# Scores of 64-wide heads read 64 rows instead of 128 zero-padded ones, and a norm is placed earlier among the top-k rounds

## Time and profile before

| | |
|---|---|
| median of three runs | 2206.35 us (2206.09 to 2206.84) |
| the profiled execution | 2206.82 us |
| its span in the trace | 2205.0 us |
| TensorE matmuls busy | 2140.5 us (97%), mean granted clock 0.993 |
| TensorE weight loads busy | 1748.2 us (79%) |
| VectorE busy | 1294.4 us (59%) |
| ScalarE busy | 871.9 us (40%) |
| GpSimd busy | 162.4 us (7%) |

### The profile page before, as it was taken

The page is one execution under the profiler, slowest core; times in us unless marked ns, Lnnn a source line. Parts: engine busy times, 40 slices in busy tenths (PEclk is TensorE's granted clock), DMA queues, the critical chain, the costliest instruction groups (busy, mean ns, idle before and its releaser), DMA issues.

```text
span 2205.0 us, 31360 instructions
## 1 busy us (share of the span) xinstructions
PE 2140.5 (97%) x10498; PEld 1748.2 (79%) x10498; DVE 1294.4 (59%) x2291; ACT 871.9 (40%) x1659; POOL 162.4 (7%) x96
## 2 busy tenths in 40 slices
PE   7998999999999999999999999999999999999997
PEld 6577778888888878888888888888888887777775
DVE  7887555666643566466666435555544457556663
ACT  4444453322223266533322332222222355455652
POOL 0042001000001111020000122000000110000001
PEclk9999999999999999999999999999999999999998
DMA  4122102233333311123332333333233334300002
GB/s 161 48 87 59 57 29 86 96 96 99 99 96 105 103 41 38 42 94 105 95 95 95 99 111 96 95 95 96 96 102 97 95 89 133 104 20 20 20 11 76
DMA packets 49472, 180.83 MB, mean 82 GB/s; under 512 B 5488, under 2 KB 5616, under 8 KB 49264
## 3 DMA queue, kind: packets, MB, share of 16 engines
q1 hardware_dynamic: 49248, 179.25, 26.0%
q0 software_dynamic: 144, 0.52, 0.1%
HBM read 177.66 MB, written 2.10 MB: 82 GB/s over the span
## 4 chain that ended last, share of the span: by engine, by line
PE 83%; DVE 4%; ACT 3%; issue 2%; DVEq 0%; POOLq 0%; ACTq 0%; POOL 0%
PE pj L2178 69%; PE po L2540 3%; PE ps L2500 2%; PE po L2395 2%; PE pt L2515 2%; PE ps L2349 2%; PE pt L2365 1%; DVE rtmp L1437 1%; ACT w_both L716 1%; DVE s_sb L1490 1%; PE pj L2318 1%; PE po L2404 0%; PE ps L2489 0%; ACT pT L830 0%; DVE w_both L1300 0%
## 5 line engine op out<-in xcount | busy, mean ns | idle before, releaser
L2178 PE MATMUL pj<-h_hi,w_both 128*128 128x512 f32 x3472 | 1121.8, 396 | 17.1 <-DVE w_both L1300 13.7
L2178 PEld LDWEIGHTS pj<-h_hi,w_both 128*128 128x128 f32 x3472 | 653.9, 188 | 156.8 <-issue 16.1
L2178 PE MATMUL pj<-h_lo,w_both 128*128 128x512 f32 x1736 | 677.4, 390 | 0.0
L716 ACT ACTIVATE w_both<-raw 128x1024 fp32r<-128x1024 f32 x321 | 340.0, 1059 | 820.6 <-PE pj L2178 811.5
L1300 DVE TENSOR_TENSOR w_both<-raw,w_both 128x1024 fp32r<-128x1024 f32 x296 | 400.0, 1351 | 303.5 <-ACT w_both L716 303.2
L2178 PE MATMUL pj<-G_hi,w_both 128*128 128x512 f32 x1408 | 440.4, 392 | 3.4 <-DVE G_lo L1649 2.2
L2178 PEld LDWEIGHTS pj<-h_lo,w_both 128*128 128x128 f32 x1736 | 327.3, 189 | 64.7 <-issue 1.4
L2178 PEld LDWEIGHTS pj<-G_hi,w_both 128*128 128x128 f32 x1408 | 264.9, 188 | 62.0 <-DVE w_both L1300 4.6
L2178 PE MATMUL pj<-G_lo,w_both 128*128 128x512 f32 x704 | 274.6, 390 | 0.0
L2178 PEld LDWEIGHTS pj<-G_lo,w_both 128*128 128x128 f32 x704 | 132.5, 188 | 26.6
L628 POOL TENSOR_TENSOR ssum<-sq 128x512 f32<-128x512 f32 x6 | 9.2, 1533 | 1439.1 <-ACT sq L953 1439.1
(11 more groups left out here) (335 smaller groups left out, 2324.0 us busy)
## 6 DMA issues: line engine op xcount, KB each, us to landing
raw<-in_wstream SPq DMA_DIRECT2D x330, 512.0 KB, 3.5
xT<-in_x SPq DMA_DIRECT2D x4, 512.0 KB, 8.5
out_x<-xT SPq DMA_DIRECT2D x4, 512.0 KB, 2.7
memT<-in_mem SPq DMA_DIRECT2D x1, 1024.0 KB, 12.2
cst<-in_cst SPq DMA_DIRECT2D x1, 512.0 KB, 10.3
tab<-in_tab POOLq DMA_DIRECT2D x1, 512.0 KB, 5.3
posi<-in_pos SPq DMA_DIRECT2D x1, 256.0 KB, 2.8
vec<-in_vec SPq DMA_DIRECT2D x1, 182.5 KB, 2.4
```

Source lines behind the costliest of these rows:

```text
L716: nc.scalar.activation(w_hi[:, c.par * CW:(c.par + 1) * CW], raw[:, c.par * CW:(c.par + 1) * CW], ACT.Copy).then_inc(hi_ready, 1)
L2178: mm = nc.tensor.matmul(acc, w[:, col:col + P], x[part], start=first and k == 0, stop=last and k == 2)
```

## The change

- Index, local and memory scores contract over the 64 partitions of their head: `rows` picks them from the query and the keys. The keys are no longer kept twice with zeros: `kidx` is one copy, `mem_k` one copy per chunk, `b_k` has both halves of a key head in the same columns. The memset of `b_k` and VectorE's wait for it are gone.
- The units of these attentions alternate between the heads (0, 1, 0, 1, ...); in the index the blocks run 1, 2, 3, 1, 2, 3 as before while the head alternates.
- The tiles of `bq` are written out one by one instead of in a loop.
- `apply("ckv")` comes after ten rounds instead of twelve; the number of rounds is the same.
- ScalarE makes the latent's high half in the last memory chunk's step, ahead of the wait for the last transpose.

```diff
-IDX_UNITS = [(hh, b) for hh in range(2) for b in range(1, NB)]
+IDX_UNITS = [(u % 2, 1 + u % 3) for u in range(6)]
-    pair = [(hh, b) for hh in range(2) for b in range(NB)]
+    pair = [(hh, b) for b in range(NB) for hh in range(2)]
...
-            if ph.name == "aq":
+            if ph.name in ("aq", "bq"):
                 for j in range(ph.tiles):
                     tile(ph, 0, j)
                 return
...
             pool.wait_ge(x_ready, RESIDUALS["down0"] + DT)
-            nc.gpsimd.memset(b_k[:, :], 0.0).then_inc(zeroed, 1)
             splits("bq")
...
                     if k < 2:
-                        act.wait_ge(chunk_used, c.v + 3)
-                        for hh in range(2):
-                            last = nc.scalar.activation(mem_k[l][:, (2 * k + hh) * MEM:(2 * k + hh + 1) * MEM],
-                                                        pj[t.par][:, 0:MEM], ACT.Copy, scale=V("half", hh))
-                        last.then_inc(pj_free[t.par], 1)
+                        take(mem_k[l][:, k * MEM:(k + 1) * MEM], t, c, n=MEM)
                     else:
                         take(vraw[:, 0:MEM], t, c, n=MEM)
+                        if l == 1 and k == 3:
+                            norm_hi("ckv")
                         act.wait_ge(v_turned, number + 1)
...
-            norm_hi("ckv")
             attention("aq")
...
-                        col = ((2 * pair + g) * 2 + hh) * S
+                        col = (2 * pair + g) * S
...
-            for hh in range(2):
-                last = nc.vector.tensor_scalar(kidx[:, hh * S:(hh + 1) * S], ktmp[:, S:2 * S], V("half", hh), None,
-                                               ALU.mult)
-            last.then_inc(roped, 1)
+            nc.vector.tensor_copy(kidx[:, 0:S], ktmp[:, S:2 * S]).then_inc(roped, 1)
...
-            rounds(5)
+            rounds(3)
             apply("ckv", lambda: rounds(1))
+            rounds(1)
             for part in range(2):
                 query(ATT["aq"], 0, 0, part)
-            rounds(TOPK // 8 - 13)
+            rounds(TOPK // 8 - 12)
...
-            dve.wait_ge(zeroed, 1)
...
+                rows = slice(0, P) if branch == "topk" else slice(hh * 64, hh * 64 + 64)
...
-                    k_at = (2 * t + hh) * MEM
-                    keys = mem_k[0 if ph.name == "amem" else 1][:, k_at:k_at + MEM]
+                    keys = mem_k[0 if ph.name == "amem" else 1][rows, t * MEM:(t + 1) * MEM]
                 elif branch == "band":
-                    keys = b_k[:, sl(g * 2 * S + hh * S + k0, w)]
+                    keys = b_k[rows, sl(g * S + k0, w)]
...
-                nc.tensor.matmul(ps[u % 2][:, 0:w], q[:, par * S + b * P:par * S + (b + 1) * P], keys,
+                nc.tensor.matmul(ps[u % 2][:, 0:w], q[rows, par * S + b * P:par * S + (b + 1) * P], keys,
...
-                    nc.tensor.matmul(ps[u % 2][:, 0:w], qs[:, j * S + b * P:j * S + (b + 1) * P],
-                                     kidx[:, hh * S:hh * S + w], start=True, stop=True).then_inc(score_done, 1)
+                    rows = slice(hh * 64, hh * 64 + 64)
+                    nc.tensor.matmul(ps[hh][:, 0:w], qs[rows, j * S + b * P:j * S + (b + 1) * P],
+                                     kidx[rows, 0:w], start=True, stop=True).then_inc(score_done, 1)
```

More of the change, by code:

```diff
@@ L1147, in _ @@
             pieces = [(which, part) for which in range(2) for part in range(2)]
-            act.wait_ge(zeroed, 2)
+            act.wait_ge(zeroed, 1)
             def window_hi(k):
@@ L1213, in _ @@
                     act.wait_ge(v_turned, TN["cmpv"] + 1)
-                    act.wait_ge(zeroed, 3)
+                    act.wait_ge(zeroed, 2)
                     for b in range(NB):
@@ L1443, in spread_keys @@
                     for hh in range(2):
-                        col = ((2 * pair + g) * 2 + hh) * S
-                        last = nc.vector.tensor_copy(dst[hh * 64:hh * 64 + 64, col:col + S], ktmp[g * 64:g * 64 + 64, pair * S:(pair + 1) * S])
+                        col = (2 * pair + g) * S
+                        last = nc.vector.tensor_copy(dst[hh * 64:hh * 64 + 64, col:col + S],
+                                                     ktmp[g * 64:g * 64 + 64, pair * S:(pair + 1) * S])
                 return last
```

## The result

The changed kernel takes 2257.23 us (median of 4 runs, 2251.47 to 2261.28), the kernel before 2206.60 beside it: a ratio of 1.0223, 95% interval 1.0201 to 1.0245. That is 50 us slower. I had forecast 30 us slower with an upper end of 2246, so the direction was right and the size missed above the range. Its runs spread over 10 us. Those of before lie within 2 us here, and within 10 as well where 23 of them were taken (2202.42 to 2211.92).

A forecast was written before the change was run, and what follows sets the result against it. TensorE, busy 97% of the span, was taken as the bound. Index +7.5, local +19.5, memory +8.1 and norm -5.0 summed to +30 us on 2206.82, forecast 2236 us, range 2217 to 2246 (8 in 10).

The forecast's parts named there:

- Price of the change of shape: Lone 64-row score among 128-row products: 0.39 us extra between projections, 0.29 between values and transpose, 0.35 between projection and transpose.
- Local attention: Layer two's 64 local scores: 62 stand alone at 0.35 us, less 2.2 covered by waits, +19.5 us (15 to 24).
- Index scores: The 48 index scores: 1.5 us per tile in four tiles, 0.8 in the last two, +7.5 us (4 to 12).
- Memory attention, twice: Both memory attentions: 14 of 16 units each stand alone at 0.29 us, +8.1 us (6 to 10).
- The clock gives way: Index or memory stages: more gaps bring more 1.2 GHz stretches, 2.7 us each, four giving 2247 us; chance 0.06.
- Norm: Latent's norm two rounds sooner: the 4.81 us stall and half clock behind it go, -5.0 us (-7.5 to -3).
- Edits at nothing: Single index-key copy, fewer memory-key copies, removed memset, unrolled local tiles: no time; up to 2 us if the memset's cover fails.
- Free: All 64-row scores: weights load under the running projection, nothing added, side-by-side scores gain, 2195 us; chance 0.10.
- half swallowed: Local and index stages: waits give more room, or only one seam is paid, about +15 - 5 + 2, 2218 us; chance 0.10.

The follow-up runs named there:

- e5: The changed kernel with only the 48 index scores put back on 128 zero-padded rows, units in the new order: 2242.20 us, ratio 1.0153.
- e4: The changed kernel with only the local attention's 64 scores put back on 128 zero-padded rows: 2236.12 us, ratio 1.0148.
- e3: The changed kernel with only the second memory attention's 32 scores put back on 128 zero-padded rows: 2238.59 us, ratio 1.0143.
- e2: The kernel before with the norm sooner, the new order of units and the local tiles written out, all scores over 128 rows: 2202.39 us, ratio 0.9980.
- e12: The kernel of e2 with only the local attention's 64 scores in 64-row form: 2218.44 us, ratio 1.0044.
- e14: The kernel of e6 with four unread 128-row products filling the stall behind the second memory attention's first scores: 2202.76 us, ratio 0.9982.
- e6: The kernel of e2 with only the second memory attention's 32 scores in 64-row form: 2219.88 us, ratio 1.0054.
- e13: The kernel of e2 with TensorE waiting behind each of 14 second-memory-attention scores until it is finished, all over 128 rows: 2206.18 us, ratio 1.0003.
- e1: The kernel before with only the norm two rounds sooner and the latent's high half ahead of the last turn: 2203.39 us, ratio 0.9986.
- e10: The kernel of e2 with only the first memory attention in 64-row form: 2204.88 us, ratio 0.9996.
- e9: The kernel of e6 with an unread second product on the other 64 rows ahead of each second-memory-attention score: 2219.51 us, ratio 1.0060.

## Why the prediction was right in direction and too small

The 50 us come together from parts that were timed by themselves: index 15.4 (e5), local 16.6 (e4), second memory attention 17.7 (e3), first memory attention 3.5 (trace), norm and order -4.4 (e2), sum 48.8. The first three are uncertain by some 6 us each, so a sum this close is partly luck. In the profiles the parts are 10.4, 15.1, 20.5, 3.5 and -6.0, sum 43.5, where the two spans differ by 44.5; the changed kernel's profiled run was its fastest.

- **Price of the change of shape.** I took 0.39 between projections, 0.29 between values and transpose, 0.35 in the local stage. All three stand: 0.39 (1.29 instead of 0.90), 0.29 (1.39 instead of 1.10) and 0.345 (1.228 instead of 0.883). My picture of the array emptying at each change of the row count was incomplete, since the passes of one score, both over 64 rows, are apart by the same 0.1.
- **Local attention.** Forecast +19.5 (15 to 24), measured +15.1 in the profile, 16.6 and 14 timed (e4, e12). The unit was right; 62 x 0.345 is 21.4, so some 6 us were swallowed where I took 2.2 off. TensorE's idle time in the windows fell by those 2.2 (3.25 to 1.04 us), its waits by 2.0 (4.7 to 2.7). The other 4 us don't show as idle time, and I have not accounted for all of them; some lie where the kernel before starts a product late while the record ahead still runs, as at 855.10, where the transpose came 0.66 behind the score instead of 0.43.
- **Index scores.** Forecast +7.5 (4 to 12), 10.4 in the profiles of e5 and the changed kernel (first index score to first top-k score, 141.1 and 151.5 us), 15.4 timed. Tile by tile the seams are as forecast: at full clock the third and the sixth tile grew by 1.44 and 1.65 us (9.52 to 10.96, 9.42 to 11.07), and the two that wait for VectorE by 0.12 each. The first seven tiles together took 78.56 us instead of 75.06, and 76.16 in e5, both of which lost a little to short stretches at half clock there. So 2.4 of the 10.4 lie in them, and the other 8.0 behind, where the stretch of 20.5 us at half clock lies. I had named it in the term's bounds ("above if the stretches at half clock grow") and not priced it.
- **Memory attention, twice.** This is the step that failed. "28 x 0.29 = +8.1" took the clock as full: the first attention lost 3.5 in the profile, near the 4.1 computed, the second 20.5, because the clock fell for 41 us. The cause stood in my rival "The clock gives way", with a chance of 0.06 and four stretches of 2.7 us. One stretch cost 16 (20.5 less 4.1 of seams; e14 is 17 us faster than e6). My argument against it was that the last attention changes shape as often at full clock; but there a projection streams between the units, and in the memory attention none does. The local stage, with a projection in every unit, bears this out: it has the seams and kept its clock (e12). e6, e13 and e14 show what I should have asked of the stage: it begins with TensorE idle for 1.7 us, and then comes a chain of short products with gaps of 0.1. Stall and 64-row scores together held the clock down in every run (e6); without the stall it never fell (e14), and without the 64-row scores it came back after 3.4 us (e2).
- **Range.** The upper bounds of the terms add up to +43, which is 2249, not the 2245 that I wrote. 2257 lies above both.
- **Norm.** Forecast -5.0 (-7.5 to -3), e1 -6.0 in the profile and -3.1 timed. The twelve products began without a wait. The first exponential came 72.3 us behind the last index score instead of 77.1, 4.8 sooner where I had 3.6: the table load of 1.28 ran at 186.55, ahead of the bias (188.33), and not behind it. The rotation was held up by 1.2 us, as I had allowed.
- **Edits at nothing.** Order, unrolling and the rest cost nothing (e2).
- **Rivals.** "Free" is refuted by the loads' rows, "half swallowed" by e4: the local stage alone paid 15.1 of some 21 us.

Open: why the first memory attention keeps its clock in most runs and the second in none (the wait ahead of it is shorter, 0.72 us against 1.67, but one profile with 0.72, e10's, fell too); which wait at the end of the index stage goes with its stretch (filling that one was not tried); and why gaps of the same length in 128-row form held the clock down in at most a third of the runs (e13) where the 64-row scores did in all (e6).

## What to carry to other kernels

In this kernel a lone product over 64 rows among products over 128 gains nothing and exposes a weight load ahead of it, between its passes and behind it; zero-padding to 128 rows is the cheaper form unless a second product on the other half can stand beside it without making another engine late. Price a change of TensorE's stream not only by the time it adds but by where it adds gaps: behind a stall, in a stage without long products, 0.3 us per unit went with half the clock for 37 to 41 us. A few products that nobody reads, put into such a stall, are a cheap test for this. Here they were also a remedy for that part of the loss; the changed kernel with them is still 1.5% slower than the kernel before.

## What was not expected of the hardware

- Half clock can go on in dense work: in the changed kernel it went on for 4.4 us of gapless projection (960.7 to 965.2 us), at the end of a stretch of 41 us.
- Idle rows are not what lets the clock fall: with both halves working (e9) it fell as with one (e6), 2219.5 and 2219.9 us.
- A product on the other 64 rows runs beside its neighbour: it starts 7 ns after it, and two scores with companions follow each other as without (e9).
- The same program falls into one behaviour or another from run to run: by time and clock, e10 twice in twelve runs and e13 four times in twelve, e6 in all five and e14 in none of twelve.
